# HGRN scores up to level 5 as 64x64 blocks in two column halves, and HGRN's queue times a quarter of a turn later

## What is computed

```
def step(s, inp):
    qq, kk, vv, ff = inp
    bc = jnp.cumsum(ff, axis=-2)
    o_inter = jnp.einsum('nbhcd,nbhde->nbhce', qq * jnp.exp(bc), s)
    diff = bc[..., :, None, :] - bc[..., None, :, :]
    decay = jnp.where(causal, jnp.exp(jnp.where(causal, diff, 0.0)), 0.0)
    scores = jnp.einsum('nbhtd,nbhsd,nbhtsd->nbhts', qq, kk, decay)
    o = o_inter + jnp.einsum('nbhts,nbhse->nbhte', scores, vv)
    blast = bc[..., -1:, :]
    s_new = jnp.exp(blast[..., 0, :])[..., None] * s + jnp.einsum(
        'nbhsd,nbhse->nbhde', kk * jnp.exp(blast - bc), vv)
    return s_new, o
```

## Time and profile before

| | |
|---|---|
| median of 3 runs | 5453.29 us (5440.58 to 5463.15) |
| the profiled execution | 5497.27 us, its span 5495.7 us |
| granted TensorE clock over the span | 0.903 |
| the stage of the two scans | about 1655 to 3390 us of the span |

### The profile page before, as it was taken

One profiled execution on the slowest core, in us unless ns is written; L12 is line 12 of the kernel. 1 busy time (PEld: TensorE's weight loads), 2 busy tenths in 40 slices (PEclk: granted clock), 3 DMA queues, 4 the chain that ended last, 5 costly groups with the idle time before them and its releaser, 6 DMA issues. The chain is left out here.

```text
span 5495.7 us, 117808 instructions
## 1 busy us (share of the span) xinstructions
PE 4415.6 (80%) x44706; PEld 3081.4 (56%) x44706; DVE 2379.1 (43%) x4070; ACT 1179.8 (21%) x3029; POOL 1560.5 (28%) x1933
## 2 busy tenths in 40 slices
PE   3989787878778888888888886778399999999950
PEld 1878655555557878788887875444133333333320
DVE  1121256465655555555555554888211111111138
ACT  0010133333323333333333332222000000000000
POOL 0000011101115555454555543443322222222110
PEclk7999898999888999999999998888699999999985
DMA  9221287878762232323223233432575888998854
GB/s 307 108 75 51 75 171 144 177 140 167 142 139 79 70 84 68 87 68 87 58 64 85 68 87 111 141 124 98 189 296 221 333 355 350 370 373 331 359 237 187
DMA packets 441527, 916.88 MB, mean 167 GB/s; under 512 B 257153, under 2 KB 296449, under 8 KB 408097
## 3 DMA queue, kind: packets, MB, share of 16 engines
q1 hardware_dynamic: 386240, 760.25, 44.4%
q0 software_dynamic: 47392, 133.02, 7.5%
q10 hardware_dynamic: 7488, 17.83, 0.9%
HBM read 951.35 MB, written 211.26 MB: 212 GB/s over the span
## 5 line engine op out<-in xcount | busy, mean ns | idle before, releaser
L2384 PE MATMUL exp_gate_up<-exp_w_gate,exp_rows_and_rowsT 128*64 128x512 f32 x1664 | 760.6, 615 | 93.3 <-DMA exp_w_up<-in_moe_w_up_dram 92.4
L2384 PE MATMUL exp_gate_up<-exp_w_up,exp_rows_and_rowsT 128*64 128x512 f32 x1664 | 761.4, 616 | 0.0
L2384 PEld LDWEIGHTS exp_gate_up<-exp_w_gate,exp_rows_and_rowsT 128*64 128x64 f32 x1664 | 233.1, 142 | 584.5 <-issue 584.3
L1525 POOL TENSOR_TENSOR rw_A_level<-rw_A_rho_beta,const_level_masks 128x256 f32<-128x256 f32 x432 | 342.8, 806 | 749.5 <-DVE rw_A_rho_beta L1541 514.0
L709 PE MATMUL rwp_product<-rwp_hT,rwp_w_rw 128*128 128x256 f32 (+1 forms) x2016 | 443.7, 383 | 0.0
L861 PE MATMUL hgp_product<-hgp_hT,const_w_hg 128*128 128x256 f32 x1728 | 411.3, 395 | 16.0 <-DMA hgp_hT<-s_hT 15.9
L2338 DVE TENSOR_TENSOR exp_hidden<-exp_hidden,exp_gate_up 64x512 f32<-64x512 f32 x104 | 71.9, 692 | 813.0 <-ACT exp_hidden L2319 813.0
L709 PEld LDWEIGHTS rwp_product<-rwp_hT,rwp_w_rw 128*128 128x128 f32 (+1 forms) x2016 | 380.8, 189 | 61.1
L861 PEld LDWEIGHTS hgp_product<-hgp_hT,const_w_hg 128*128 128x128 f32 x1728 | 340.1, 200 | 76.3 <-DMA hgp_hT<-s_hT 16.3
L2408 PE MATMUL exp_down<-exp_w_down,exp_hiddenT 128*64 128x512 f32 x1664 | 380.0, 598 | 1.1
L1556 DVE TENSOR_TENSOR rw_inverse<-rw_inverse,rw_inverse_bank 128x512 f32<-128x512 f32 x288 | 197.7, 686 | 287.5 <-PE rw_inverse_bank L1435 287.5
(11 more groups left out here) (379 smaller groups left out, 8194.0 us busy)
## 6 DMA issues: line engine op xcount, KB each, us to landing
exp_w_gate<-in_moe_w_gate_dram SPq DMA_DIRECT2D x104, 2048.0 KB
exp_w_up<-in_moe_w_up_dram SPq DMA_DIRECT2D x104, 2048.0 KB
exp_w_down<-in_moe_w_down_dram SPq DMA_DIRECT2D x104, 2048.0 KB
rw_operands<-s_rw_in SPq DMA_DIRECT2D x72, 514.0 KB, 5.5
rw_tokens<-s_rw_tm SPq DMA_DIRECT2D x144, 192.0 KB, 6.5
hg_qkf<-s_hg_in SPq DMA_DIRECT2D x36, 768.0 KB, 8.0
mod_w<-in_w_mod_dram SPq DMA_DIRECT2D x24, 1024.0 KB, 26.1
prep_raw<-s_rw_lat SPq DMA_DIRECT2D x16, 1536.0 KB
```

Of the source, the lines that this page charges most:

```text
L1525: nc.gpsimd.tensor_tensor(self.al[d][l % 2][:], self.ar[u][d][:, :, 0, :], self.K["lvc"][:, d, l, :].unsqueeze(1).broadcast_to([P, NPAIR, ...
L2384: i = nc.tensor.matmul(pgu[u][q:q + BLK], xT[:, k, r * BLK:(r + 1) * BLK], w[r][:, k, :], start=(k == 0), stop=(k == KD - 1))
```

## The change

The score tile of each direction shrinks from [128, 4, 128] to [128, 4, 64]: partition s of the upper half keeps only targets 0 to 63, one of the lower half only 64 to 127. For tasks 0 to 13 PE makes the two diagonal 64x64 blocks of each head with two matmuls of a 128x64 tile each, on the left and the right half of the array's columns, with 64 moving columns; DVE combines them with masks of 64 columns (`K["lvc"]`, `K["idc"]`, which exist already for RWKV). Tasks 14 and 15 make the one block across with one such matmul and DVE copies it into the half of a new tile, `scores_across`, whose other half stays at the zeros that a memset at the start puts there. In the output the product with the 128x128 scores becomes three: a 128x64 one with `scores_across` and a 64x64 one for each diagonal block. An addition to the semaphore `turns` goes ahead of each task on PE. All of HGRN's times, on ACT, POOL, PE and DVE, are moved from 0 to 1 of the turn to 0.25 to 1.25.

```
@@ both_scans @@
-            side_by_side(two, h(eng, k, u))
+            side_by_side(two, shifted(h(eng, k, u), 0.25, 1.0))
@@ HgrnScan @@
+HALF = (slice(0, RW_C), slice(RW_C, P))
-        self.sc = [sb(f"scores{d}", [P, HH, P]) for d in range(2)]
+        self.sc = [sb(f"scores{d}", [P, HH, RW_C]) for d in range(2)]
+        self.sc6 = [sb(f"scores_across{d}", [P, HH, RW_C]) for d in range(2)]
-        self.psc = [ps(f"score_psum{r}", [P, HH, P]) for r in range(2)]
+        self.psc = [ps(f"score_psum{r}", [P, HH, P])[:, :, 0:RW_C] for r in range(2)]
@@ pe, scores @@
-                for h in range(HH):
-                    mm = nc.tensor.matmul(self.psc[t % 2][:, h, :], self.qkf[u][d][:, 1, h, :], self.qkf[u][d][:, 0, h, :], start=True, stop=True)
+                k, q = self.qkf[u][d][:, 1], self.qkf[u][d][:, 0]
             else:
                 pe.wait_ge(s["z_ready"], 14 * n + t - 1)
-                for h in range(HH):
-                    mm = nc.tensor.matmul(self.psc[t % 2][:, h, :], self.z[r][:, h, :], self.z[r][:, h, :], start=True, stop=True)
+                k, q = self.z[r], self.z[r]
+            pe.sem_inc(s["turns"], 1)
+            for h in range(HH):
+                for a, b in ((0, 0), (1, 1)) if t < 14 else ((d, 1 - d),):
+                    mm = nc.tensor.matmul(self.psc[t % 2][HALF[a], h, :], k[:, h, HALF[a]], q[:, h, HALF[b]], start=True, stop=True)
@@ pe, output @@
             if d == 0 and isinstance(n, int) and n == 0:
-                pe.wait_ge(s["state_zero"], 2)
+                pe.wait_ge(s["state_zero"], 4)
...
-                mm = nc.tensor.matmul(self.po[:, h, :], self.sc[d][:, h, :], self.v[u][d][:, h * P:(h + 1) * P], start=False, stop=True)
+                v = self.v[u][d][:, h * P:(h + 1) * P]
+                nc.tensor.matmul(self.po[HALF[1 - d], h, :], self.sc6[d][:, h, :], v, start=False, stop=False)
+                for a in range(2):
+                    mm = nc.tensor.matmul(self.po[HALF[a], h, :], self.sc[d][HALF[a], h, :], v[HALF[a]], start=False, stop=True)
@@ dve, combine_scores @@
-                nc.vector.tensor_tensor(self.sc[d][:], self.psc[t % 2][:], K["ident"][:].unsqueeze(1).broadcast_to([P, HH, P]),
+                nc.vector.tensor_tensor(self.sc[d][:], self.psc[t % 2][:], K["idc"][:].unsqueeze(1).broadcast_to([P, HH, RW_C]),
                                         ALU.mult).then_inc(s["combined"], 1)
+            elif t < 14:
+                dve.sem_inc(s["turns"], 1)
+                nc.vector.copy_predicated(self.sc[d][:], K["lvc"][:, d, t // 2 - 1, :].bitcast(U32).unsqueeze(1).broadcast_to([P, HH, RW_C]),
+                                          self.psc[t % 2][:]).then_inc(s["combined"], 1)
             else:
-                dve.sem_inc(s["turns"], 1)
-                nc.vector.copy_predicated(self.sc[d][:], K["lvl"][:, d, t // 2 - 1, :].bitcast(U32).unsqueeze(1).broadcast_to([P, HH, P]),
-                                          self.psc[t % 2][:]).then_inc(s["combined"], 1)
+                wait(dve, s["out_done"], 2 * (n - 1) + d + 1)
+                nc.vector.tensor_copy(self.sc6[d][HALF[d]], self.psc[t % 2][HALF[d]]).then_inc(s["combined"], 1)
@@ scans, at DVE's start @@
                     nc.vector.memset(h.st[d][:], 0.0).then_inc(h.s["state_zero"], 1)
-                dve.wait_ge(h.s["state_zero"], 2)
+                    nc.vector.memset(h.sc6[d][:], 0.0).then_inc(h.s["state_zero"], 1)
+                dve.wait_ge(h.s["state_zero"], 4)
```

## The result

The changed kernel takes 5395.1 us against 5458.2 for the kernel before, both as medians on one chip: a ratio of 0.9892, interval 0.987 to 0.9915. That is the forecast's number, 5395, and the interval is clear of 1.

The account below looks back on a forecast made before the run. PE was taken to bound the scan stage, idling at step turns; tiles -2.3, DVE -0.3 and shift -0.3 make -2.9 us a step, 18 steps -52, plus -6 once: 5453 - 58 = 5395 us, range 5290 to 5500.

Parts of the forecast that it names:

- The second rival: Score tiles on PE: halves don't overlap at 64 columns, a pair costs 125 ns, singles 100; 5506 us, chance 0.15.
- 24 changes are 2.4 us: HGRN's output on PE: tile shape changes three times a head, about 0.1 us each, 2.4 us a step.
- PE's net: Score and output tiles on PE: scores save 6.6 us a step, the output gives back 4.3, net -2.3.
- (a): Loop's end on PE: code fetch no longer behind the loads, gap 6.1 to 2.5 us; with (b) -4.0 a step.
- (b): Middle of the loop body: RWKV's mask no longer behind logf, 4.39 us wait goes; with (a) -4.0 a step.
- (c): Gram matmuls behind the two gaps: half clock goes, 3.68 us against 1.96, -1.8 us a step.
- (d): POOL: HGRN's scaled copies stop competing with RWKV's first levels, PE's waits for L408 and lost clock go, -2.0 a step.
- The 6 us once in the first turn: First turn: PE's 5.84 us wait for a mask behind HGRN's scan goes, -6 us once.
- Together +7.5: The shift's costs to PE, (e), (f) and (g) summed: 7.5 us a step given back, leaving the shift -0.3.
- (f): HGRN's 5.4 us ACT burst stands ahead of RWKV's copy of X for level 3: 4 us idle, 1 for clock.
- (e): RWKV runs alone on PE for a third of the turn: 2 us idle a step.
- (g): HGRN's outputs at the turn's end have no RWKV beside them on PE: 0.5 us a step.

Follow-up runs that it names:

- the kernel with column halves, the cheap output and later ends: Changed kernel with scores written as blocks into a full tile, the output's single 128x128 product of before, and HG_ENDS 0.095 instead of 0.045: ratio 0.9757 to before.
- the fastest kernel: Changed kernel with the single-product output of before, HG_ENDS at 0.095 and the loop over the turns written out: ratio 0.9597 to the kernel before.

## Why the prediction was right, and where it was not

**What bounds the kernel.** Right. The mask queued behind HGRN's scan and the code behind the loop's jump were the two causes; each went when its cause was taken away (the shift, and the loop written out), and the packet of code was late behind the loads, as the prediction read it.

**The scores.** The pair costs 66 ns where I took 75, and the scores fell by 7.0 to 7.5 us a step, predicted 6.6. The second rival is refuted. In the Trainium skill "TensorE: Matmul & The Clock Gate", section "What overlaps and what doesn't", has a weight load overlap a running matmul only when their row groups differ. Here 64 columns at two cycles each are 53 ns of stream at 2.4 GHz; a pair that shares its rows and loads twice in 66 ns has no room for loads of its own, so the trace does not agree with the strict form of the rule.

**The output.** Mis-sized: "24 changes are 2.4 us" and 1.9 for the products, 4.3 together. Measured 6.0 on top of the shift and 5.4 without it. One output has (4.58 - 2.85) / 12 = 0.14 us a change of shape, not 0.09, if the products themselves cost the 2.85 that the prediction's prices give (1.89 and four times 0.24). PE's net of the tiles in the changed kernel is thus -7.0 + 6.0 + 0.5 = -0.5 us, not -2.3.

**DVE.** 5.8 us less work a step, predicted 4.3, and no gain that can be seen: with 2.6 us PE waits for it more than with the shift alone (2.2), where 0.3 less was predicted. The price of an entry in a queue, "under 0.1", is borne out for PE by the 59 ns.

**The shift, what it takes away.** (a) and (b), -4.0: measured 47.0 / 17 = 2.8 for the mask and 1.5 for the loop's end, 4.2 together. (c) -1.8: RWKV's own time fell by 2.1, though 5 of the 7 gram groups behind the loop's end still run at lower clock (2.4 to 3.6 us). (d) -2.0: POOL's wait 1.4, and 0.9 at L1412, which the prediction did not name. The sizes of all are right. The 6 us once in the first turn did not come: that wait for the mask went, but from the first gram matmul to the end of the first HGRN step it is 91.4 us instead of 90.3.

**The shift, what it gives back.** This is the step that failed: "Together +7.5". Measured for (f), ACT's burst, are 2.3 where the prediction had 4, and its 1 more for the clock can't be told apart, since the mean clock rose from 0.95 to 0.97; for (e), RWKV alone on PE, 1.1 more wait of L1424 for DVE where it had 2; of (g), 0.5, nothing is seen. That is some 3.4 in place of 7.5. So the shift alone is worth -5.9 us a step and not -0.3.

**The sum.** -2.9 a step was predicted, -2.65 measured, but as -5.9 for the shift and +3.2 for the tiles on top of it. The number was met by luck. Of the +3.2, -0.5 is PE's net, and the rest I had not foreseen: 1.8 of stops that nothing named ends, 0.7 of slower RWKV work, and waits for tokens and DVE. The prediction had a code fetch at the loop's end alone and none inside the turn. By the packets, the stops of 1 us or more that wait for code make 20.9 us in the 17 steps of the shift alone and 37.3 in the changed kernel, 1.0 us a step more; in the kernel with column halves, the cheap output and later ends they make 73.0, and 31.0 with its loop written out, 2.5 of the 5.0 us a step that this edit gives. (The 50.3 us of L428 in the fastest kernel, which nothing named ends, are the wait for POOL that has 37.1 with the loop.) That code comes late more often when PE gets faster or has more instructions is what these kernels show; why, is open.

## What to carry to other kernels

Two edits that each fill or remove the same wait don't add: time each alone before they go in together, even when the sum comes out as forecast. Put a burst that sits ahead of a critical short copy in a queue behind it; that was worth 0.008 of the ratio here, where the whole change gave 0.011. When a product is cut into smaller tiles, count the changes of tile shape in everything that reads the result, and keep the consumer in one shape, if another engine has time to put the blocks in place. When PE stops and the profile names nothing, look for instruction packets among the DMA transfers just ahead of its start.

## What the runs showed of the hardware that I had not expected

- A change of tile shape on PE costs an estimated 0.14 us in a row of short groups (three a head in the output, 4.58 us where 2.85 are work by the prices of the prediction), 0.09 between long ones.
- A sem_inc in PE's queue between matmuls costs about 59 ns, 256 of them 15 us a step, and 3 us of short stops besides.
- Behind the jump of a long loop PE lost 2.5 us and then 1.3 and 1.5 within the next 16 us, none of it named by the profile, each 1.4 to 1.8 us behind the end of a 16 KB packet of code; with the loop written out the same kernel was 5.0 us a step faster.
- Two column halves that share all row groups, with 64 moving columns, take 66 ns a pair.
